# Shifting the large SBUF buffers by 96 bytes a partition in a one-core hybrid decoder layer

## What is computed

```
h = rms_norm(x, norm_mix_g)
proj = h @ w_in                      # 4096 mixer columns and 3 * 2048 gate columns
o_a = hgrn2_mixer(...)               # gated linear recurrence
o_b = s5_mixer(...)                  # diagonal state space, then a GLU
o_c = stick_breaking_mixer(...)      # causal attention, 128-query blocks
merged = sum of sigmoid(gate_k) * (o_k @ w_branch[k]), k = a, b, c
x = x + merged @ w_out
hf2 = rms_norm(x, norm_ffn_g)
up = causal_depthwise_conv(hf2 @ w_up, conv_w)            # width 3
x = x + (silu(up[..., :5632]) * up[..., 5632:]) @ w_down
```

## Time and profile before

| | us |
|---|---|
| median of 3 runs | 1403.05 (1402.94 to 1403.38) |
| the profiled execution | 1402.92 |
| its span in the profile | 1401.4 |
| PE busy | 1394.3 (99%) |
| PE weight loads busy | 1285.5 (92%) |
| DVE busy | 1030.6 (74%) |
| ACT busy | 754.0 (54%) |
| POOL busy | 143.4 (10%) |
| DMA, mean over the span | 187 GB/s |

### The profile page before, as it was taken

One profiled execution on the slowest core, in us unless ns is written; L12 is line 12 of the kernel. 1 busy time (PEld: TensorE's weight loads), 2 busy tenths in 40 slices (PEclk: granted clock), 3 DMA queues, 4 the chain that ended last, 5 costly groups with the idle time before them and its releaser, 6 DMA issues.

```text
span 1401.4 us, 27481 instructions
## 1 busy us (share of the span) xinstructions
PE 1394.3 (99%) x9682; PEld 1285.5 (92%) x9682; DVE 1030.6 (74%) x1409; ACT 754.0 (54%) x1050; POOL 143.4 (10%) x190
## 2 busy tenths in 40 slices
PE   9999999999999999999999999999999999999999
PEld 8999999999999999988888888888888888888888
DVE  7898866699898777776687777777777776445453
ACT  7584777654543454545555555555555554344332
POOL 1200000000000014322111111111111110000000
PEclk9999999999999999999999999999999999999999
DMA  8654545454555556665556656656656656666663
GB/s 280 191 181 168 162 153 184 147 168 165 189 178 174 195 171 223 223 192 194 170 197 196 189 186 192 192 180 193 191 187 193 190 177 194 208 185 202 194 206 109
DMA packets 75935, 261.66 MB, mean 187 GB/s; under 512 B 8736, under 2 KB 9280, under 8 KB 75872
## 3 DMA queue, kind: packets, MB, share of 16 engines
q1 hardware_dynamic: 74304, 256.41, 57.0%
q0 software_dynamic: 1424, 4.37, 1.1%
q10 hardware_dynamic: 144, 0.01, 0.0%
HBM read 258.66 MB, written 2.10 MB: 186 GB/s over the span
## 4 chain that ended last, share of the span: by engine, by line
PE 91%; DVE 6%; ACT 2%; DMA 1%; issue 0%; SPq 0%; ACTq 0%; DVEq 0%
PE bank L354 40%; PE bank L368 22%; PE bank L356 21%; PE bank L394 5%; DVE w_lo L1024 2%; PE pair L413 1%; PE bank L379 1%; DVE a_in L1257 0%; ACT gates L721 0%; ACT w_hi L711 0%; DMA x_first<-xT 0%; DVE tmp L1055 0%; DVE tmp L1048 0%; DVE x_first L1217 0%; ACT tmp L721 0%
## 5 line engine op out<-in xcount | busy, mean ns | idle before, releaser
L1024 DVE TENSOR_TENSOR w_lo<-raw,w_hi 128x1024 fp32r<-128x1024 f32 x496 | 584.6, 1189 | 305.3 <-ACT w_hi L711 301.5
L711 ACT ACTIVATE w_hi<-raw 128x1024 fp32r<-128x1024 f32 x496 | 508.3, 1030 | 417.0 <-PE bank L356 198.9
L354 PE MATMUL bank<-h,w_hi 128*128 128x512 f32 x1408 | 488.4, 390 | 0.0
L356 PE MATMUL bank<-h,w_lo 128*128 128x256 f32 x1408 | 397.1, 282 | 0.0
L368 PE MATMUL bank<-a_in,w_hi 128*128 128x256 f32 x2048 | 363.1, 281 | 0.5 <-DVE w_lo L1024 0.5
L368 PEld LDWEIGHTS bank<-a_in,w_hi 128*128 128x128 f32 x2048 | 311.8, 188 | 5.3 <-issue 4.6
L354 PEld LDWEIGHTS bank<-h,w_hi 128*128 128x128 f32 x1408 | 264.2, 188 | 55.4
L368 PE MATMUL bank<-a_in,w_lo 128*128 128x256 f32 x1024 | 285.5, 279 | 0.0
L356 PEld LDWEIGHTS bank<-h,w_lo 128*128 128x128 f32 x1408 | 266.1, 189 | 0.0
L354 PE MATMUL bank<-act,w_hi 128*128 128x512 f32 x660 | 228.8, 390 | 0.0
L368 PEld LDWEIGHTS bank<-a_in,w_lo 128*128 128x128 f32 x1024 | 192.5, 188 | 0.0
(11 more groups left out here) (222 smaller groups left out, 1370.3 us busy)
## 6 DMA issues: line engine op xcount, KB each, us to landing
raw<-w_up SPq DMA_DIRECT2D x176, 512.0 KB, 3.8
raw<-w_in SPq DMA_DIRECT2D x156, 512.0 KB, 4.3
raw<-w_down SPq DMA_DIRECT2D x80, 512.0 KB, 4.2
raw<-w_out SPq DMA_DIRECT2D x32, 512.0 KB, 4.2
raw<-w_br SPq DMA_DIRECT2D x16, 512.0 KB, 3.5
raw<-w_br SPq DMA_DIRECT2D x16, 256.0 KB, 3.4
raw<-w_down SPq DMA_DIRECT2D x16, 256.0 KB, 2.7
x_first<-xT SPq DMA_DIRECT2D x8, 256.0 KB, 6.6
```

What stands on the lines that cost most here:

```text
L354: pe.matmul(bank[b][:, :], w[:, k * P:(k + 1) * P], a.rearrange("p a t -> p (a t)"), start=first and n == 0, stop=False, skip_group_check= ...
L356: mm = pe.matmul(bank[b][:, 0:SEQ], l[:, k * P:(k + 1) * P], a[:, 0, :], start=False, stop=last and n == len(blocks) - 1, skip_group_check ...
L711: act_e.activation(w_hi[s][:, 0:blocks * P], raw[s][:, 0:blocks * P], ACT.Copy).then_inc(hi_ready, 1)
L1024: ve.tensor_tensor(w_lo[s][:, w], raw[s][:, w], w_hi[s][:, w].bitcast(F32), ALU.subtract).then_inc(lo_ready, 1)
```

## The change

One tile is taken from the stack behind `root`, and nothing reads or writes it:

```diff
@@ -159,6 +159,7 @@
         rstd = sb("rstd", [P, SEQ])
         var = sb("var", [P, SEQ])
         root = sb("root", [P, SEQ])
+        sb("apart", [P, 24])
 
 
         late = ExitStack()
```

## The result

The changed kernel takes 1419.45 us (median of 4 runs, 1419.34 to 1420.26) against 1402.99 us for the kernel before on the same chip: a ratio of 1.0119, 95% interval 1.0107 to 1.0131. It is slower by 16.5 us, where 60 us less were forecast. The profiled execution's span is 1417.8 us, 16.4 more than before.

What follows compares the result with a forecast made beforehand. PE's matmul count times pitch was taken as the bound: 44.0 us saved on pairs and 19.6 on triples, 63.6 together, so 1403.05 - 63.6 + 3.8 given back = 1343 us, range 1328 to 1409.

Steps and rivals of the forecast that it cites:

- What bounds the kernel: Whole kernel: PE busy 1394.3 of 1401.4 us and fed nearly everywhere; time is the number of matmuls times their pitch.
- the part that grows with the columns goes: All F32R matmuls: aligned activations save 17.7 ns a pair, 4.7 a triple's matmul, together 63.6 us; chance 0.42.
- an excess: F32R matmuls at full rate: 10.0 ns (256 columns) and 16.6 (512) over the clock, 6.5 per 256 columns plus 3.5 fixed.
- The floor of the weight loads: 256-column matmuls: each needs its 128x128 weight load, so the pitch stops at 112 ns instead of 110.2.
- One line less: Rival, all 9132 matmuls: alignment saves one 128-byte line, 0.83 ns each, 7.6 us, giving 1395.4 us; chance 0.15.
- Nothing: Rival, F32R matmuls: the excess stays whatever the address, or 32 bytes is alignment enough; 1403 us; chance 0.25.
- Slower: Rival, all 9132 matmuls: aligned weights and activations read at once disturb each other, 1.1 ns each, 10 us, 1413; chance 0.18.
- the evidence: Input projection: nine triples of the same 256-column matmuls at 117.8 ns each, against 116.7 elsewhere.
- the point of decision: All matmuls: the slower rival decides the sign from 0.3 ns more a matmul on (2.8 us).
- its argument against itself: 512-column matmul: its second half has no weight load beside it yet shows 6.5 ns, so most excess isn't a collision.
- What is late next: DVE, splitting each piece, must keep up: 1.8 us given back from 60 to 100 us, 2 us more in bursts.
- The 5% of the forecast: Up projection: at 5% less time DVE, busy 312 of 400 us, would be at 82%.

Runs made afterwards that it cites:

- Short loads: Test matmuls behind the last product of the kernel before, F32R streams of 128 to 512 columns with 32-column weight loads: 256 columns 117.3 ns, 512 columns 231.6.
- second grid: Test matmuls behind the kernel before's last product, 8 distances of high weights by 8 of low: pairs 339.8 ns at 64 and 0, 353.5 at 224 for both.
- The fastest kernel: Kernel before with padding between w_hi and w_lo and behind root, every activation tile 64 from high and 0 from low weights: 1389.61 us, ratio 0.9903.
- pair of crossed runs: Against the kernel before: all tiles moved 96 bytes, weights included, 1402.94 us; weights and activations both at 32 past a multiple of 128, 1420.05 us.
- the kicks: Test series of 20 pairs behind the kernel before's last product, each after one odd matmul of 64 to 232 columns: 352.8 and 348.9 ns at distance 64.

## Why the prediction was wrong

**What bounds the kernel** was right, and it carried the whole study. PE is fed nearly everywhere, and the time is the number of matmuls times the pitch. The counts, 2484 pairs and 4164 matmuls of triples, turned the measured pitches into microseconds to within 3 us in every run.

**The failed step** is "I take as forecast that the part that grows with the columns goes". That there is an excess, that it grows with the columns and that it belongs to F32R at full rate was right. Its size was less sure than the text made it: the 6.5 ns for 256 columns stood on a 256-column matmul costing the same in a pair as in a triple. The starts give 118.3 ns in a pair, against 116.7, and 228.4 for the 512-column one, against 229.9. Short loads give 7.7 ns for 256 columns (0.030 a column). What I added, that a start off a multiple of 128 bytes makes it, had no F32R row behind it, as the text said. All that stood for it was the float32 difference between `eye` and `tmp`, a transpose against a product, and the fact that the excess could be counted in units of 128 bytes. Pairs were to take 328.9 ns; they took 351.1, because the distance from the weights, which the sum did not hold, went from 32 to 128. No alignment tried, at any of 16 distances or in the second grid's 64 combinations, brought a pair below 339.8.

**The floor of the weight loads**, 112 ns, never came into play in the kernel: the lowest rhythm seen is 113.3. Loads of 32 columns let 256 columns go no faster than 113.3 either, so the length of the load does not seem to set that value.

**One line less** would have been 345 ns a pair; the pitch rose. **Nothing** was wrong as well. By the 16-byte lines of the Trainium skill (SBUF — State Buffer, Specifications), which the prediction set beside this rival, a shift by a multiple of 16 touches no more lines; yet steps of 16 bytes change the pitch by up to 6.6 ns (144 to 160 in the pairs, 96 to 112 in the triples).

**Slower** was the rival that came true, at a chance of 0.18. It named the place (weights and activations read at once), the evidence (one form in two rhythms) and the point of decision. Its price was too low: 1.1 ns for each of 9132 matmuls, 10 us. Measured were 2.2 for each matmul of a pair and 1.7 to 3.3 in the triples, 16.5 us, so the result lies also above the range. And its argument against itself misled me: that the second half of a 512-column matmul has no load beside it. No row showed that. The trace lists the load for 0.19 us of the 0.22 between the two starts:

```profile
899.96 0.19 PEld L356 LDWEIGHTS bank<-h,w_lo 128*128 128x128 f32 x1
900.19 0.19 PEld L354 LDWEIGHTS bank<-h,w_hi 128*128 128x128 f32 x1
```

From the loads of 128 and 32 columns (188 and 108 ns) the part that grows with the columns can be estimated at 107 ns, which would leave the second half free, but that came with the experiments. Even so it would not follow that the load's place is harmless. It need not make the excess to decide in which rhythm the stream runs.

**What is late next** wasn't tested, since PE did not become faster. The fastest kernel shows only that DVE keeps up with a small gain: at 1.9% more matmuls in the long stretch it is busy 317 of 400 us. The 5% of the forecast were never reached.

**What stays open.** That the distance decides is shown by the pair of crossed runs, that there are several rhythms by the kicks. What in PE locks, and why the period is 256 bytes, is not. Bank conflicts between the two reads would fit the period, but the short loads speak against the simplest form of that. A stream without loads, which would tell how much of the excess is the stream's own, is missing, and distances were tried only in steps of 16 bytes.

## What to carry to other kernels

Where PE streams 4-byte operands at full rate and is never idle, read the pitch and not the busy share: about 2% hung on where the tiles stand here (1389.61 to 1420.68 us). What counts is the distance between weights and moving operand modulo 256 bytes, not the alignment of either, so a tile added between the two can move such a kernel by a per cent in either direction, while one ahead of both did nothing. Measure the distances in test matmuls at the end of the kernel, several times each behind a different start, since one distance may have more than one rhythm.

## What the runs showed of the hardware that was not expected

- The pitch of the same two F32R matmuls with their loads lies between 339.8 and 353.7 ns by the distances and the rhythm alone, with the other engines at rest, at a granted clock of 1.00.
- At one distance several pitches can be stable; a single matmul of odd length switches between them (348.9 and 353.3 for pairs at 64, 113.3 and 117.8 for triples at 192, 340.0 and 350.0 at 64 and 0).
- An F32R stream costs 0.447 ns a column with weight loads of 32 columns beside it; a bf16 stream of 256 columns takes 109.4 ns in all.
- Moving every tile by 96 bytes, weights included, costs nothing that can be measured (1.0001, interval 0.9991 to 1.0010).
